# Which of two weight buffers a seven-product pair is loaded into, and where its tiles lie there

## What is computed

```python
D_MODEL = 1024
D_FF = 2816

def swiglu_ffn(x, w_in, w_out):
    g, u = jnp.split(x @ w_in, 2, axis=-1)
    return (jax.nn.silu(g) * u) @ w_out
...
for i in range(4):
    ...                                   # mixer of layer i, added to xp and xs
    xp = xp + swiglu_ffn(rmsnorm(xp, ffn_norms[i]), *ffn_params[i])
    xs = xs + swiglu_ffn(rmsnorm(xs, ffn_norms[i]), *ffn_params[i])
```

## Time and profile before

| | |
|---|---|
| median of three runs | 2651.1 us (2649.98 to 2657.7) |
| profiled execution, its own time | 2653.51 us |
| its span in the trace | 2651.8 us |
| mean granted clock of TensorE | 0.995 |
| TensorE matmul busy | 2596.8 us, 98%, 20353 matmuls |
| TensorE weight load busy | 2524.9 us, 95% |
| VectorE busy | 1549.6 us, 58% |
| ScalarE busy | 1114.0 us, 42% |
| GpSimd busy | 171.0 us, 6% |
| read from HBM | 219.03 MB, 86 GB/s over the span (with 8.87 MB written) |

### The profile page before, as it was taken

One profiled execution on the slowest core, in us unless ns is written; L12 is line 12 of the kernel. 1 busy time (PEld: TensorE's weight loads), 2 busy tenths in 40 slices (PEclk: granted clock), 3 DMA queues, 4 the chain that ended last, 5 costly groups with the idle time before them and its releaser, 6 DMA issues.

```text
span 2651.8 us, 48473 instructions
## 1 busy us (share of the span) xinstructions
PE 2596.8 (98%) x20353; PEld 2524.9 (95%) x20353; DVE 1549.6 (58%) x2225; ACT 1114.0 (42%) x1682; POOL 171.0 (6%) x182
## 2 busy tenths in 40 slices
PE   8999999999999999999999999999999999999998
PEld 8999999999988999999998899999999999999998
DVE  5655773765555577467556556746745555773442
ACT  5454441433555554233345635423434543541233
POOL 2101000001000100000112210000011101000001
PEclk9999999999999999999999999999999999999999
DMA  3223232332433232332322232333232222332232
GB/s 114 69 73 88 78 101 76 96 99 77 124 101 103 76 88 80 104 96 75 93 73 77 66 92 80 80 103 86 74 89 85 70 80 81 96 92 80 83 98 78
DMA packets 440519, 230.55 MB, mean 87 GB/s; under 512 B 15780, under 2 KB 436864, under 8 KB 440336
## 3 DMA queue, kind: packets, MB, share of 16 engines
q1 hardware_dynamic: 438688, 226.89, 30.5%
q10 hardware_dynamic: 1200, 0.59, 0.1%
q0 software_dynamic: 448, 0.45, 0.1%
HBM read 219.03 MB, written 8.87 MB: 86 GB/s over the span
## 4 chain that ended last, share of the span: by engine, by line
PE 82%; DVE 8%; DMA 5%; ACT 2%; issue 1%; SPq 0%; DVEq 0%; ACTq 0%
PE slot L2244 56%; PE slot L2723 9%; PE aux L2723 8%; DMA raw<-in_l_ffn_w_in_dram 5%; PE aux L2212 2%; DVE w_lo L1380 2%; ACT w_hi L710 1%; DVE ffn_w_sums L2008 1%; PE aux L2244 1%; DVE w_lo L2019 1%; PE aux L2625 1%; DMA raw<-in_l_ffn_w_out_dram 1%; PE aux L2389 1%; PE aux L2631 1%; PE aux L2537 1%
## 5 line engine op out<-in xcount | busy, mean ns | idle before, releaser
L2244 PE MATMUL slot<-xg_hi,w_hi 128*128 128x272 f32 x2464 | 529.4, 296 | 12.7 <-DVE w_lo L1380 10.0
L2244 PE MATMUL slot<-xg_hi,w_lo 128*128 128x272 f32 x2464 | 512.1, 289 | 0.0
L2244 PE MATMUL slot<-xg_lo,w_hi 128*128 128x272 f32 x2464 | 511.7, 289 | 0.0
L710 ACT ACTIVATE w_hi<-raw 128x1024 fp32r<-128x1024 f32 (+3 forms) x279 | 315.9, 1132 | 439.3 <-PE slot L2244 318.8
L1380 DVE TENSOR_TENSOR w_lo<-raw,w_hi 128x1024 fp32r<-128x1024 f32 (+3 forms) x277 | 368.0, 1329 | 108.4 <-ACT w_hi L710 106.8
L2244 PEld LDWEIGHTS slot<-xg_hi,w_hi 128*128 128x128 f32 x2464 | 388.8, 190 | 25.2 <-DVE w_lo L1380 12.4
L2244 PEld LDWEIGHTS slot<-xg_lo,w_hi 128*128 128x128 f32 x2464 | 389.8, 190 | 0.0
L2244 PEld LDWEIGHTS slot<-xg_hi,w_lo 128*128 128x128 f32 x2464 | 388.4, 190 | 0.0
L2244 PE MATMUL slot<-h_hi,w_hi 128*128 128x272 f32 x1386 | 286.7, 288 | 4.7 <-DVE w_lo L1380 4.5
L2244 PE MATMUL slot<-h_hi,w_lo 128*128 128x272 f32 x1386 | 285.8, 287 | 0.0
L2244 PE MATMUL slot<-h_lo,w_hi 128*128 128x272 f32 x1386 | 285.5, 287 | 0.0
(11 more groups left out here) (395 smaller groups left out, 5154.7 us busy)
## 6 DMA issues: line engine op xcount, KB each, us to landing
raw<-in_l_ffn_w_in_dram SPq DMA_DIRECT2D x134, 512.0 KB, 4.0
raw<-in_l_ffn_w_out_dram SPq DMA_DIRECT2D x64, 704.0 KB, 4.7
raw<-in_l_gla_w_in_dram SPq DMA_DIRECT2D x48, 512.0 KB, 3.9
ffn_raw_b<-in_l_ffn_w_in_dram SPq DMA_DIRECT2D x42, 512.0 KB, 7.1
raw<-in_l_att_w_qkv_dram SPq DMA_DIRECT2D x24, 512.0 KB, 3.8
raw<-in_l_lru_w_in_dram SPq DMA_DIRECT2D x24, 512.0 KB, 3.8
raw<-in_l_gla_w_out_dram SPq DMA_DIRECT2D x16, 512.0 KB, 3.9
raw<-in_l_lru_w_out_dram SPq DMA_DIRECT2D x7, 768.0 KB, 4.8
```

What stands on the lines that cost most here:

```text
L710: act.activation(w_hi[par][:, 0:kt, :], raw[par][:, 0:kt, :], ACT.Copy).then_inc(s_hi, 1)
L2244: ins = pe.matmul((slot[par] if bank is None else bank)[:, hf, 0:HALF], w[par][:, k, :], a[:, k0 + k, hf * HALF:(hf + 1) * HALF], start=(k ...
```

## The change

Three things change together.

The buffers change places: `"AB"` becomes `"BA"`, so the first S pair of a run is loaded into the spare buffer and the second into `raw`. Both now wait for `s_lo >= b - 2` (for the second pair that means: the C pair before the run is wholly split).

An S pair in `raw` lies in it in another way. Its first quarter (u rows 0-3), which only the first weight sum reads (line 2008), goes into the half in which the next block will be loaded; the other three quarters go into the other half. For this its load is in three pieces: two of 256 KB and one of 512 KB, in the spare buffer too.

What follows a run waits otherwise. `after_seven` gives the two waits of the first two blocks behind an S pair. Behind one in the spare buffer both wait for the split of all before that S pair (`s_lo >= b - 2`). Behind one in `raw` the first block waits for that pair's first weight sum (`s_ws`, called `seven_w_sums` below), the second for its last split (`s_lo >= b`). The first turn of the down projection's loop of loads is taken out of the loop for this; in the down projection only the first block uses the new wait.

The counts of landed loads on ScalarE and VectorE (`raw_off` in place of `in_b`) follow the pieces. Of the edits that stand on ScalarE and on VectorE alike the diff below shows one copy.

```diff
@@ -169,7 +169,7 @@
             for u, kind in enumerate(up_kinds(i, hf, layers) or ""):
                 run = run + 1 if kind == "S" else 0
                 if run:
-                    number[i, hf, u], buffer[i, hf, u] = n, "AB"[(run - 1) % 2]
+                    number[i, hf, u], buffer[i, hf, u] = n, "BA"[(run - 1) % 2]
                     n += 1
     return number, buffer, n
 
@@ -476,7 +476,19 @@
 
         def w_raw(at):
 
-            return FF["raw_b"] if s_buf[at] == "B" else raws
+            if s_buf[at] == "B":
+                return FF["raw_b"], 0, KQ
+            return (raws, 0, KMAX) if pair_at(*at) % 2 == 0 else (raws, KMAX, 0)
+
+        def raw4(at, n):
+
+            r, _, rest = w_raw(at)
+            return tiles4(r, rest + n * KQ)
+
+        def raw_apart(at):
+
+            r, _, rest = w_raw(at)
+            return tiles_apart(r, rest)
 
         def sum_at(p0):
 
@@ -516,9 +528,18 @@
                         sp.dma_start(ST["vec_rows"][at:at + rows, v, :], src.rearrange(form, p=P)).then_inc(s_vec, 16)
                         at += rows
 
-            def load(b, par, src, kt, done=None):
+            def after_seven(i, hf, u):
+
+                if not u or up_kinds(i, hf, layers)[u - 1] == "C":
+                    return None
+                b, before = pair_at(i, hf, u), (i, hf, u - 1)
+                if s_buf[before] == "B":
+                    return (s_lo, b - 2), (s_lo, b - 2)
+                return (s_ws, 3 * s_no[before] + 1), (s_lo, b)
+
+            def load(b, par, src, kt, free=None):
                 if not (isinstance(b, int) and b < 2):
-                    sp.wait_ge(s_lo, b - 1 if done is None else done)
+                    sp.wait_ge(*(free or (s_lo, b - 1)))
                 sp.dma_start(raw[par][:, 0:kt, :], src).then_inc(s_raw[par], 16)
 
             def load_gates(g):
@@ -661,20 +682,25 @@
                         b = b0 + 2 * u
                         g_at, u_at = (hf * FH + u) * P, D_FF + (hf * FH + u) * P
                         if seven == "C":
+                            free = after_seven(i, hf, u)
                             for j, at in enumerate((g_at, u_at)):
-                                load(b + j, (b0 + j) % 2, wi[:, :, at:at + P], XT,
-                                     done=b - 2 if u and kinds[u - 1] == "S" else None)
+                                load(b + j, (b0 + j) % 2, wi[:, :, at:at + P], XT, free=free and free[j])
                             continue
-                        to_b = s_buf[i, hf, u] == "B"
-                        sp.wait_ge(s_lo, b - 2 if to_b else b)
-                        into = w_raw((i, hf, u))
-                        sp.dma_start(into[:, 0:XT, :], wi[:, :, u_at:u_at + P]).then_inc(s_rawb if to_b else s_raw[b0 % 2], 16)
-                        sp.dma_start(into[:, XT:2 * XT, :], wi[:, :, g_at:g_at + P]).then_inc(s_rawb if to_b else s_raw[1 - b0 % 2], 16)
+                        sp.wait_ge(s_lo, b - 2)
+                        (into, first, rest), p0 = w_raw((i, hf, u)), b % 2
+                        here, there = (s_rawb, s_rawb) if s_buf[i, hf, u] == "B" else (s_raw[p0], s_raw[1 - p0])
+                        sp.dma_start(into[:, first:first + KQ, :], wi[:, 0:KQ, u_at:u_at + P]).then_inc(here, 16)
+                        sp.dma_start(into[:, rest:rest + KQ, :], wi[:, KQ:XT, u_at:u_at + P]).then_inc(there, 16)
+                        sp.dma_start(into[:, rest + KQ:rest + 3 * KQ, :], wi[:, :, g_at:g_at + P]).then_inc(there, 16)
                     b0 = base[i, f"down{hf}"]
-                    with sp.Fori(0, XT // 2) as m2:
+                    def down_load(m2, free=None):
                         for j in range(2):
                             load(b0 + m2 * 2 + j, (b0 + j) % 2,
-                                 wo[:, hf * FH:(hf + 1) * FH, ds(m2 * (2 * P) + j * P, P)], FH)
+                                 wo[:, hf * FH:(hf + 1) * FH, ds(m2 * (2 * P) + j * P, P)], FH, free=None if j else free)
+                    after = after_seven(i, hf, FH) if kinds else None
+                    down_load(0, after and after[0])
+                    with sp.Fori(1, XT // 2) as m2:
+                        down_load(m2)
             y_rows = o[0].rearrange("a (t p) n -> (a p) t n", p=P)
             sp.wait_ge(s_yd, 1)
             sp.dma_start(y_rows[:, 2:3, :], EN["rows"][:, 2:3, :]).then_inc(s_yo, 16)
@@ -695,13 +721,13 @@
             act.dma_start(ST["gain_rows"][P - DEC_SEQ:P - DEC_SEQ + XT, :], d["l0_norm_mix"].rearrange("(c p) -> c p", p=P)).then_inc(s_g0, 16)
             act.dma_start(raw[0][:, 0, :].rearrange("p (k n) -> p k n", k=XT), w3("l0_gla_w_gate_a")).then_inc(s_raw[0], 16)
 
-            in_b = 0
+            raw_off = [0, 0]
 
             def split(b, par, kt):
 
                 if kt is None:
                     return
-                act.wait_ge(s_raw[par], (b - par) * 8 + (16 - 16 * in_b))
+                act.wait_ge(s_raw[par], (b - par) * 8 + (16 + raw_off[par]))
                 if not (isinstance(b, int) and b < 2):
                     act.wait_ge(s_mm, b - 1)
                 if kt == "low":
@@ -1188,13 +1214,21 @@
                         two(m2, kt)
                 two(XT // 2 - 1, next_k(i, name))
 
+            def raw_used(at, b):
+
+                if s_buf[at] == "B":
+                    for par in range(2):
+                        raw_off[par] -= 16
+                else:
+                    raw_off[1 - b % 2] += 16
+
             def raw_landed(at, b):
 
                 if s_buf[at] == "B":
-                    act.wait_ge(s_rawb, 32 * (b_no[at] + 1))
+                    act.wait_ge(s_rawb, 48 * (b_no[at] + 1))
                 else:
                     for par in range(2):
-                        act.wait_ge(s_raw[par], (b + (b % 2 != par) - par) * 8 + (16 - 16 * in_b))
+                        act.wait_ge(s_raw[par], (b + (b % 2 != par) - par) * 8 + (16 + raw_off[par] + 16 * (b % 2 != par)))
 
             def hi_sums(at, b, prev):
 
...
@@ -1222,11 +1256,9 @@
 
             def hi_rest(at, b):
 
-                nonlocal in_b
                 act.wait_ge(s_mm, b)
-                act.activation(tiles_apart(w_his, w_slots(b % 2)[5]), tiles_apart(w_raw(at), KQ), ACT.Copy).then_inc(s_hi, 2)
-                if s_buf[at] == "B":
-                    in_b += 1
+                act.activation(tiles_apart(w_his, w_slots(b % 2)[5]), raw_apart(at), ACT.Copy).then_inc(s_hi, 2)
+                raw_used(at, b)
 
             def copy_product(at, p0, which):
 
...
 
-                r, s, n, to = w_raw(at), FF["s"], 3 * s_no[at], sum_at(b % 2)
+                (r, first, rest), s, n, to = w_raw(at), FF["s"], 3 * s_no[at], sum_at(b % 2)
                 raw_landed(at, b)
-                dve.tensor_tensor(tiles8(s, to[0]), tiles8(r, KQ), tiles4(r, 0).unsqueeze(1).broadcast_to([P, 2, KQ * P]),
+                dve.tensor_tensor(tiles8(s, to[0]), tiles8(r, rest), tiles4(r, first).unsqueeze(1).broadcast_to([P, 2, KQ * P]),
                                   ALU.add).then_inc(s_ws, 1)
                 dve.wait_ge(s_ws, n + 1)
-                dve.tensor_tensor(tiles4(s, to[2]), tiles4(s, to[0]), tiles4(r, 2 * KQ), ALU.add).then_inc(s_ws, 1)
+                dve.tensor_tensor(tiles4(s, to[2]), tiles4(s, to[0]), raw4(at, 1), ALU.add).then_inc(s_ws, 1)
                 dve.wait_ge(s_ws, n + 2)
-                dve.tensor_tensor(tiles4(s, to[3]), tiles4(s, to[2]), tiles4(r, 3 * KQ), ALU.add).then_inc(s_ws, 1)
+                dve.tensor_tensor(tiles4(s, to[3]), tiles4(s, to[2]), raw4(at, 2), ALU.add).then_inc(s_ws, 1)
 
             def lo_sums(at, b):
 
@@ -2035,13 +2075,11 @@
 
             def lo_rest(at, b):
 
-                nonlocal in_b
                 to = w_slots(b % 2)[5]
                 dve.wait_ge(s_hi, b + 2)
-                dve.tensor_tensor(tiles_apart(w_los, to), tiles_apart(w_raw(at), KQ), tiles_apart(w_his, to).bitcast(F32),
+                dve.tensor_tensor(tiles_apart(w_los, to), raw_apart(at), tiles_apart(w_his, to).bitcast(F32),
                                   ALU.subtract).then_inc(s_lo, 2)
-                if s_buf[at] == "B":
-                    in_b += 1
+                raw_used(at, b)
 
             def c_plus_d(at, p0):
 
```

More of the change, by code:

```diff
@@ L1211, in hi_a11 @@
                     act.wait_ge(s_mm, b)
-                act.activation(tiles4(w_his, w_slots(b % 2)[4]), tiles4(w_raw(at), 2 * KQ), ACT.Copy).then_inc(s_wh, 1)
+                act.activation(tiles4(w_his, w_slots(b % 2)[4]), raw4(at, 1), ACT.Copy).then_inc(s_wh, 1)
             def hi_more_sums(at, b, prev):
@@ L2025, in lo_a11 @@
                 dve.wait_ge(s_wh, 3 * s_no[at] + n)
-                dve.tensor_tensor(tiles4(w_los, to), tiles4(w_raw(at), 2 * KQ), tiles4(w_his, to).bitcast(F32),
+                dve.tensor_tensor(tiles4(w_los, to), raw4(at, 1), tiles4(w_his, to).bitcast(F32),
                                   ALU.subtract).then_inc(s_wl, 1)
```

12 lines of the change are left out of this document (9 added, 3 removed).

## The result

The changed kernel takes 2619.51 us (median of 4 runs, 2617.88 to 2621.93), the kernel before 2652.32 (4 runs, 2649.98 to 2657.7): a ratio of 0.9874, 95% interval 0.9857 to 0.9892, 32.8 us less. The forecast was 2617, with 2612 to 2632 around it. The profiled execution took 2619.49 us, its span is 2617.7 us and the mean granted clock 0.996, against 2653.51, 2651.8 and 0.995.

The account below looks back on a forecast made before the run. TensorE, busy 98% of the span, was taken to bound the kernel, with pauses from late loads. Terms 27.8 + 6.3 + 0.85 = 35.0 us gave 2616.1 from the median 2651.1, 2617 with tight starts; range 2612 to 2632.

Parts of the forecast that it names:

- The 24 first starts: First seven-product pair of each run: the early spare-buffer load removes all TensorE pauses there, 27.8 us.
- The lower bound: Same 24 starts: at least 1.05 us each, taken from one period of three pairs, 25 us.
- VectorE's room: VectorE's sums, read and subtraction before a run's start: done 2.4 us before TensorE needs them, 0.6 at layers' first runs.
- The down projections: Starts of the down projections behind a seven-product pair: first load issued earlier, pauses go, 5.3 + 1 = 6.3 us.
- The second load: Second load behind every second seven-product pair: issued later, but 4.1 us to spare before ScalarE takes it, so 0 us.
- rival B: Second block behind a run of two, 17 + 4 places: its late second load makes the kernel slower than before; chance 0.03.
- More and smaller loads: SyncE: 45 more DMAs, three pieces instead of two, about 0.4 us per issue, cost 0 us.
- rival C: Spare buffer's load queued behind the late second load: the old order returns, 2648 to 2652 us; chance 0.06.
- The clock: Half-speed stretch of 3.41 us from 1814.67 behind a pause: goes with the pause, 0.85 us, bounds 0 and 1.7.
- The 0.8 us set aside for tight starts: VectorE's chain at the tightest starts, 4 first runs, gives back some 0.2 us each, which makes 2617.
- Rival A: The 24 starts: VectorE's chain replaces the load, 0.3 to 0.6 us of pause stays at each, 2624 to 2631; chance 0.18.

Follow-up runs that it names:

- e8: The kernel of e3, but the spare buffer's load waits again for the ordinary pair's last split (s_lo >= b): 2646.92 us.
- e2: The changed kernel, but the down projection's first load waits for the last split, as before the change: 2623.93 us.
- e4: The changed kernel, but an ordinary pair's second load behind a run waits until that pair's own first block is split: 2619.7 us.
- e5: The changed kernel, but an ordinary pair's second load behind a run waits until TensorE has finished the run's matmuls: 2648.26 us.
- e3: The changed kernel with the old placing in raw, two 512 KB loads per seven-product pair, and both blocks behind it waiting for its last split: 2619.65 us.
- e1: The changed kernel, its loads in three pieces, but the spare buffer's load waits as the shared one did before (s_lo >= b): 2682.0 us.
- e9: The kernel of e1, but the second pair's load into raw is held until the first pair's first weight sum has read the spare buffer: 2659.87 us.

## Why the prediction was right

The forecast, 2617 us, is 2.5 us below the median. By its steps:

1. The 24 first starts: 27.8 us were forecast, 27.7 measured. The lower bound (25, from the one period shown) was too low because that period's pause was shorter than the mean. VectorE's room was forecast at 2.4 us and is 2.5; at the first run of layer 0 it was forecast at 0.6 and is 1.0 (the subtraction ends at 303.1, TensorE starts at 304.1). e8 gives the step by itself, 27 us.
2. The down projections: 6.3 forecast, 6.5 in the trace. e2, with the old wait, loses 4.1 us of it in its trace (4.4 by the medians); the late start of the earlier trace rows pauses 2.02 us there and not 2.96, so a part of the step, 2.3 us, came without the new wait, by an earlier issue and a shorter landing whose cause stays open.
3. The second load: 0 forecast, 0 found. It is issued at 350.40 and ScalarE takes it up at 358.5; it has landed 4.2 us before that in the median, 4.1 were forecast. e4 issues it 5.8 us later still and loses nothing, e5 shows the price beyond. But the step and rival B counted the room to TensorE's next block alone. In e5 the larger part of the idle time, 13.9 of 22.9 us, sits at the next run's start, a second consumer that neither named.
4. More and smaller loads: 0 forecast, and 0 here (e3), although an issue into the spare buffer takes SyncE 0.51 to 0.58 us and not the 0.4 that was counted. But this holds only because the load has room. I had not seen that a load in three pieces lands 0.9 us later with a megabyte behind it; had the load stayed as late as in rival C, the kernel would have stood above the one before, as e1 does, and not at 2648 to 2652.
5. The clock: 0.85 us forecast. The stretch at 1.2 GHz of the earlier trace rows is gone together with the pause ahead of it, and TensorE's matmuls there are 1.55 us quicker. But the sum got nothing from it: the 34.1 us of start-to-start losses already make up the whole difference of the spans. What stands against the stretch is another one at 2240.90 in the start of layer 3, and 0.5 us by which the program's first blocks came later (the new stretch: us, busy time and instructions of the engines, PEclk, DMA share, GB/s):

```profile
2240.90:2244.30 3.40, 3.40 (x17) 3.40 (x17) 2.39 (x5) 1.66 (x3) 0.00 (x0) 0.50 0.57 168
```

Before, that layer had its stretch one pair earlier, at 2258.41, ahead of a wait for VectorE, where it cost nothing; now it follows that wait and costs about 1.5 us. So the term was within its bounds for the place it spoke of, and the clock took as much elsewhere.

The 0.8 us set aside for tight starts were not needed. That the sum comes out so close is in part luck: this allowance and the 0.85 us of the clock both came to nothing, and they cancel. What separates 2617 from 2619.5 is the base: the sum, 34.2 us with that allowance, is right within 0.2, but I had leaned to the median of three runs, 2651.1. The median of four is 2652.3, and 2652.3-34.1 = 2618.2; the rest is inside the spread of the runs.

Rival A (VectorE's chain takes the load's place) did not come: its pauses would be at line 2059, which has none. Rival B works as a mechanism (e5) and so does a late first load (e1, e8), the core of rival C; the changed kernel has neither.

## What to carry to other kernels

A late load whose wait goes through a chain of splits can be cured by taking the buffer whose last reader is done earliest; with the same loads and the same instructions that was worth 27 us, 1.0%, here (e3 against e8). Count room at every last consumer, not at the engine in between: ScalarE could wait 28.7 us more for its loads at no cost, and when it waited 69.0 us more, the nearest consumer was not the one that lost most. Set a wait against the same engine's idle time in the kernel that it is compared with, since another wait may have stood there already. Load in few pieces where the transfer ends last, as here a third piece and a megabyte queued behind each delayed the last landing; and a pause at a start costs more than its length if the clock falls behind it.

## What the runs showed of the hardware

The same megabyte from HBM on one queue landed 5.8 us after its first issue as two DMAs and 6.7 as three, with another megabyte issued behind it (e8, e1); with nothing behind it 5.6 as two (e3) and 6.2 as three (e9).

A stretch at half clock costs nothing where TensorE will wait for another engine anyway. At the third pair of a layer TensorE pauses 0.39 us by its idle time where the clock had just been at 1.2 GHz, and 1.93 where it had not:

```profile
291.98 0.49 PE L2282 MATMUL aux<-xg_hi,w_hi 128*128 128x272 f32 x2 [0.39 <-issue]
...
958.66 0.48 PE L2282 MATMUL aux<-xg_hi,w_hi 128*128 128x272 f32 x2 [1.93 <-issue]
```

```profile
278.20:281.60 3.40, 3.40 (x17) 3.40 (x16) 3.16 (x6) 2.12 (x4) 0.00 (x0) 0.51 0.61 180
```

The last row is the stretch ahead of the first of them. From the start of the second pair, where each layer pauses 2.1 us, to this matmul it is 14.21 us in the one layer (277.77 to 291.98) and 14.22 in the other (944.44 to 958.66): VectorE's chain sets this time, and the half clock only turned waiting into slow work.

Whether a pause brings the clock down is not decided by its length alone. Pauses of 1.98 us did in e1 (at 1225.63 and 1689.96), and one of 2.60 us at 2367.91 in the same execution did not. The Trainium skill ("TensorE: Matmul & The Clock Gate", the section on HAM oscillation) tells of a kernel whose short bursts of matmuls each wait longer than they last for a DMA, so that every burst starts at half clock, and says that the clock stays up where a burst is much longer than its wait. The bursts here last some 33 us; in e1's trace 3 of the 24 pauses had a stretch at half clock right behind them, so here it mostly stays up, but not always.
